# A two-block transformer kernel: the last four meetings of the engines removed, small loads moved

## The chip, the cores and the metric

The kernel runs on one core of a Trainium2 chip. The metric is device time in microseconds of one execution. The core has five engines with queues of their own: TensorE (PE), VectorE (DVE), ScalarE (ACT), GpSimd (POOL) and SyncE (SP, which here issues most of the DMA transfers). They meet only through semaphores.

## What is computed

Two blocks are applied to 512 tokens of width 1024, all in float32. The first block is a token mixer (a gated recurrence and an mLSTM), a cross-attention and a squared-ReLU MLP, then a norm. The second block is cut here to the part around the change; its expert layer follows behind it.

```python
a = rmsnorm_2(h, norm_mix[l])
proj = a @ w_in[l]
aq, ak, av, gq, gk, gv, gr, z_f, z_b, g_att, g_gla = split_columns(proj)
aq = partial_rope(aq.reshape(B, S, ATT_HEADS, ATT_HEAD_DIM), positions)
ak = partial_rope(ak.reshape(B, S, ATT_KV_HEADS, ATT_HEAD_DIM), positions)
y_att = windowed_gqa(aq, ak, av, attn_sink[l]) @ w_branch_attn[l]
y_gla = gla_branch(gq, gk, gv, gr, z_f, z_b, gla_gate_up_fwd[l], ...) @ w_branch_gla[l]
merged = jax.nn.sigmoid(g_att) * y_att + jax.nn.sigmoid(g_gla) * y_gla
h = h + merged @ w_out[l]
```

`partial_rope` turns the first 16 of each head's 64 values by sine and cosine of position times eight frequencies. `z_f` and `z_b` are 16 columns each of the projection; `gla_branch` multiplies them by the small `up` weights, and the result is the log decay of each token.

## The kernel before

**Products and their weights.** Each large product runs over panels of 512 weight columns, and a panel is cut into parts of two row tiles (256 rows, 512 KB). A float32 value is written as an upper part in the matmul's rounded format and a remainder, and a product is three matmuls (upper by upper, upper by remainder, remainder by upper). One part takes 24 matmuls of 128x512. SP loads parts into four raw buffers (`raw`, L2483); a raw buffer is loaded again as soon as its part is split. The split writes the upper half and the remainder into one of two slots. In most stages POOL does both (L580 and L581, in `split_parts_of`). In `proj_h` and `proj_m`, ACT copies the upper half (L590, `split_hi`) and POOL subtracts (L599, `split_lo`). A slot is free when PE has used the part two before. So splitting runs two parts ahead of PE at most, and `early(name)` splits the first two parts of a stage, `rest(name)` the others.

**PSUM banks.** Eight banks carry all results. A table (`STAGES`) gives every result its bank; PE claims it when its former content has been read (`bank_claim`), and an engine that evacuates it waits until it is written. `bank_written` and `bank_done` are these waits alone. Some stages use only the left or only the right four banks, so that weights' products (`product_steps`, one step is one group of a part, six matmuls) can be put between the small matmuls of another stage.

**The norm before the second block** (`final_mix_act`, `final_mix_dve`, `fused_pe`). DVE adds each bank of the MLP's result to X (L485) and multiplies by a gain (L486: both inputs lie in SBUF), ACT squares and sums, DVE scales (L496), PE transposes (L457), ACT and DVE evacuate into the split input XTS. Then follow `proj_a` (queries, keys, values of the attention), the `z` product with the padded and split weights ZWS (L625), eight steps of `proj_g`, six transposes of the turned queries and keys (`turn_qk`, L2003), the attention with the other steps of `proj_g` and `proj_v` between (`attn_pe`: scores L1381, transposes L1387, outputs L1394), the alpha products with `gatt` between (L2013), `yatt`, and the gated linear attention with `proj_r` between (`gla_pe`, L1488 its first product of each chunk).

**The meetings.** `Stages` (L186) is a barrier of PE, ACT, DVE and POOL: each drains its pipeline, raises `stage_end` and waits until all four have come (L194). There are four: after `z`; after `turn_qk`; after the attention; after `yatt`. Between the first two, DVE computes the angles, ACT their sine and the sine of half of them (L2165, L2166), DVE the cosine, then it turns queries and keys. The scratch of this lies where the attention's scores come later.

**POOL's order.** At the start: clear `small` and `ident`, split two parts of `proj_h`, issue four loads of bias rows `bc`, the sink and the positions, set masks, clear WG and issue four loads of four columns each into it, then go on splitting. Before the second block POOL waits until PE has done the last transpose of the norm, clears ZW, issues two loads of 16 columns each into it and two of `up` weights, and then splits `proj_a` (L1909 to L1916). At the meetings it has split two parts of the next stage.

Of the kernel before, what the change touches and what calls it, by code (L numbers as in the profile page):

```python
# [13 lines left out]
ALU = mybir.AluOpType  # L14
ACT = mybir.ActivationFunctionType
# [65 lines left out]
def build(nc, ctx, A, out):  # L81
# [28 lines left out]
    PT = sb("PT", [P, 2, P])  # L110
    bc = sb("bc", [P, 2048])
# [23 lines left out]
    stage_end = sem("stage_end")  # L135
# [47 lines left out]

    met = []

    class Stages:  # L186

        def __init__(self, eng):
            self.eng, self.n = eng, 0
            met.append(self)  # L190

        def __call__(self):
            self.n += 1
            self.eng.drain().then_inc(stage_end, 1)  # L194
            self.eng.wait_ge(stage_end, 4 * self.n)

# [1081 lines left out]
    CS_, SN_ = a.take(ST, 8), a.take(ST, 8)  # L1278
    RT = a.take(4, ST, 8, 8)
    ANG = a.take(4, ST, 8)  # L1280
# [554 lines left out]
    def _(pool):  # L1835
        meet = Stages(pool)
# [61 lines left out]
        pool.wait_ge(S_("wg_in"), 64)  # L1898
# [33 lines left out]
        early("proj_r")  # L1932
        meet()
        rest("proj_r")
# [8 lines left out]
    def _(pe):  # L1943
        meet = Stages(pe)
# [48 lines left out]
        meet()  # L1993
# [11 lines left out]
        meet()  # L2005
        attn_pe(pe, steps)
        meet()
# [11 lines left out]
        meet()  # L2019
# [62 lines left out]
    def _(act):  # L2082
        meet = Stages(act)
# [73 lines left out]
        final_mix_act(act, BASE["down1"])  # L2157
        act.wait_ge(S_("x_final"), 1)
# [3 lines left out]
        meet()  # L2162

        act.wait_ge(S_("ang"), 1)
        act.activation(SN_[:, :, :], ANG[:, 0], ACT.Sin)  # L2165
        act.activation(CS_[:, :, :], ANG[:, 0], ACT.Sin, scale=0.5).then_inc(S_("sin"), 1)  # L2166
# [4 lines left out]
        meet()  # L2171
        attn_act(act)
        meet()
# [13 lines left out]
        meet()  # L2187
        act.wait_ge(S_("x_kept"), 16)
        gla_act(act, link)
# [280 lines left out]
    def _(sp):  # L2470
# [14 lines left out]
        for p in range(late):  # L2485
            load(p)
# [56 lines left out]
```

## Time and profile before

| | us |
|---|---|
| median of three runs | 2175.28 (2175.22 to 2177.37) |
| the profiled execution | 2175.02 |
| its span | 2173.2 |
| PE busy | 1997.0 |
| DVE busy | 784.0 |
| ACT busy | 532.9 |
| POOL busy | 1029.3 |

The times of the profile are those of one execution, counted from the start of its span. A line of the timeline has start, duration, engine, source line, operation, what it writes and reads, and in brackets how long its engine was idle before it and what ended that. A line of the windows has a stretch, its length, the busy time of PE, of its weight loads (PEld), of DVE, ACT and POOL (with instruction counts), then PE's granted clock as a share of full speed, the DMA engines' busy share and GB/s. The list of waits gives who waited for whom, then total, number and longest.

### The profile page before, as it was taken

How to read it: one execution, taken by the hardware profiler on the slowest of the kernel's cores; microseconds unless marked ns; L12 is line 12 of the kernel's file. 1: busy time of each engine (PE TensorE's matmuls, PEld its weight loads, DVE VectorE, ACT ScalarE, POOL GpSimd, SP SyncE). 2: the span in 40 equal slices, each digit the busy share in tenths (PEclk: the TensorE clock that was granted, in tenths of full speed). 3: DMA queues.
4: the chain of work that ended last, by engine and by line, in shares of the span. 5: the costliest groups of instructions: out<-in, count | busy, mean ns of one | idle time of the engine just before them, and what ended most of it. 6: DMA issues, size and time to landing. Idle time of an engine off the chain costs nothing.

```text
span 2173.2 us, 23270 instructions
## 1 busy us (share of the span) xinstructions
PE 1997.0 (92%) x9424; PEld 1449.9 (67%) x9424; DVE 784.0 (36%) x1186; ACT 532.9 (25%) x1119; POOL 1029.3 (47%) x596
## 2 busy tenths in 40 slices
PE   7988997978989999997999999988979999999977
PEld 6877886767778888886766667877854444434436
DVE  1445558442323301424144374553240111111135
ACT  3434436322312100212023242332120000000032
POOL 6786747736466877885643385445600000000015
PEclk9999998999999999998999999999979999999998
DMA  5321112312222333331311122112659999999971
GB/s 159 97 62 36 40 59 78 127 40 87 68 70 76 97 97 97 97 97 57 112 49 59 49 62 83 57 51 67 244 194 387 409 409 409 409 409 409 409 288 58
DMA packets 116922, 334.89 MB, mean 154 GB/s; under 512 B 8145, under 2 KB 9873, under 8 KB 116561
## 3 DMA queue, kind: packets, MB, share of 16 engines
q1 hardware_dynamic: 111904, 319.97, 40.9%
q10 hardware_dynamic: 4128, 11.60, 1.5%
q0 software_dynamic: 784, 1.84, 0.3%
q8 instruction: 75, 1.23, 0.2%
q14 instruction: 31, 0.25, 0.0%
HBM read 327.10 MB, written 6.29 MB: 153 GB/s over the span
## 4 chain that ended last, share of the span: by engine, by line
PE 78%; DVE 6%; POOL 6%; DMA 5%; ACT 3%; issue 2%; POOLq 1%; PEldq 0%; SPq 0%; DVEq 0%; ACTq 0%; PEld 0%
PE bank L556 47%; PE bank L1709 12%; PE bank L1739 3%; PE bank L1726 2%; PE bank L718 2%; POOL shared_r L580 2%; DMA shared<-in_w_exp_gate 2%; POOL shared_r L581 2%; PE bank L457 1%; PE bank L1381 1%; DMA arena<-in_w_exp_up 1%; DMA arena<-in_w_exp_gate 1%; DMA shared<-in_w_exp_down 1%; PE bank L1394 1%; POOL shared_r L599 1%
## 5 line engine op out<-in xcount | busy, mean ns | idle before, releaser
L556 PE MATMUL bank<-shared_r 128*128 128x512 f32 (+1 forms) x4032 | 962.7, 395 | 41.0 <-POOL shared_r L581 18.8
L556 PEld LDWEIGHTS bank<-shared_r 128*128 128x128 f32 x4032 | 746.3, 194 | 217.0 <-issue 26.9
L580 POOL TENSOR_TENSOR shared_r<-shared,small 128x1024 fp32r<-128x1024 f32 (+1 forms) x184 | 355.3, 1931 | 992.3 <-DMA shared<-in_w_ple_gate 530.7
L581 POOL TENSOR_TENSOR shared_r<-shared,shared_r 128x1024 fp32r<-128x1024 f32 (+1 forms) x184 | 455.4, 2475 | 14.5
L648 DVE TENSOR_TENSOR X<-bank,X 128x512 f32<-128x512 f32 x96 | 66.4, 692 | 427.8 <-PE bank L1726 240.8
L1709 PE MATMUL bank<-shared,arena 128*64 128x512 f32 x864 | 191.3, 594 | 10.6 <-DMA shared<-in_w_exp_gate 4.0
L556 PE MATMUL bank<-shared_r,arena_r 128*128 128x512 f32 x768 | 176.1, 391 | 0.0
L556 PEld LDWEIGHTS bank<-shared_r,arena_r 128*128 128x128 f32 x768 | 144.2, 188 | 31.5
L1709 PE MATMUL bank<-arena 128*64 128x512 f32 x672 | 149.2, 594 | 6.6 <-DMA arena<-in_w_exp_gate 2.0
L1709 PEld LDWEIGHTS bank<-shared,arena 128*64 128x64 f32 x864 | 67.4, 137 | 129.7 <-issue 119.9
L599 POOL TENSOR_TENSOR shared_r<-shared,shared_r 128x1024 fp32r<-128x1024 f32 x32 | 80.5, 2516 | 79.8 <-ACT shared_r L590 79.8
L1709 PEld LDWEIGHTS bank<-arena 128*64 128x64 f32 x672 | 51.9, 137 | 98.7 <-issue 90.2
L718 PE MATMUL bank<-arena 128*128 128x64 f32 x448 | 60.9, 286 | 15.9 <-DVE arena L863 12.3
L2155 ACT ACTIVATE arena<-arena 128x512 f32<-128x512 f32 x32 | 20.2, 632 | 224.8 <-DVE arena L2311 224.3
L718 PEld LDWEIGHTS bank<-arena 128*128 128x128 f32 x448 | 60.6, 206 | 19.7 <-DVE arena L863 13.5
L556 PE MATMUL bank<-arena_r,shared_r 128*128 128x512 f32 x288 | 67.7, 395 | 0.8 <-issue 0.8
L1739 PEld LDWEIGHTS bank<-arena 128*128 128x128 f32 x512 | 60.4, 199 | 9.0 <-issue 7.9
L1739 PE MATMUL bank<-arena 128*128 128x128 f32 x512 | 61.7, 284 | 3.0 <-issue 1.9
L556 PEld LDWEIGHTS bank<-arena_r,shared_r 128*128 128x128 f32 x288 | 53.8, 187 | 14.3 <-issue 1.2
L2311 DVE TENSOR_SCALAR arena<-bank 128x512 f32<-128x512 f32 x32 | 21.9, 685 | 113.6 <-PE bank L556 113.2
L1777 ACT ACTIVATE arena<-bank 128x512 f32<-128x512 f32 x16 | 8.8, 595 | 218.3 <-PE bank L1763 218.2
L1726 PE MATMUL bank<-arena 128*128 128x512 f32 x128 | 56.8, 597 | 2.1 <-issue 2.1
(392 smaller groups left out, 2030.2 us busy)
## 6 DMA issues: line engine op xcount, KB each, us to landing
shared<-in_w_in SPq DMA_DIRECT2D x80, 512.0 KB, 3.6
shared<-in_w_exp_up SPq DMA_DIRECT2D x38, 1024.0 KB, 18.3
shared<-in_w_exp_down SPq DMA_DIRECT2D x36, 1024.0 KB, 18.6
shared<-in_w_exp_gate SPq DMA_DIRECT2D x34, 1024.0 KB, 18.2
arena<-in_w_exp_gate SPq DMA_DIRECT2D x30, 1024.0 KB, 18.5
arena<-in_w_exp_down SPq DMA_DIRECT2D x28, 1024.0 KB, 18.3
arena<-in_w_exp_up SPq DMA_DIRECT2D x26, 1024.0 KB, 18.2
shared<-in_w_up SPq DMA_DIRECT2D x32, 512.0 KB, 3.7
```

Of the source, the lines that this page charges most:

```text
L457: ins = pe.transpose(bank[:, j * P:(j + 1) * P], XS[:, j, d * P:(d + 1) * P], ident[:, :])
L556: ins = pe.matmul(dst, W_, x_, start=first, stop=final)
L580: link(pool.tensor_tensor(hi, raw(p), small[:, 18:19].to_broadcast([P, hi.shape[1]]), ALU.add))
L581: pool.tensor_tensor(lo, raw(p), hi.bitcast(F32), ALU.subtract).then_inc(S_("w_split"), 1)
L599: pool.tensor_tensor(lo, raw(p), hi.bitcast(F32), ALU.subtract).then_inc(S_("w_split"), 1)
L648: bank_release(dve.tensor_tensor(xs, bank[:, :], xs, ALU.add), n)
L718: ins = pe.matmul(bank[:, h * 64:(h + 1) * 64], HKL[g % 4][:, h, :], HQL[g % 4][:, h, :], start=True, stop=True)
L1381: ins = pe.matmul(bank[:, lo:hi], QT[r, hp, x * P:(x + 1) * P], KTT[r, g, (x - 1) * P + lo:(x - 1) * P + hi], start=True, stop=True)
L1709: ins = pe.matmul(banks_[h][x_rows(e), :], stay, panel[:, kk, h * 512:(h + 1) * 512], start=k == 0, stop=k == KT - 1)
L1726: bank_ready(pe.matmul(bank[:, :], AOH[i % 2][:, 1, j * P:(j + 1) * P], YP[:, h * 512:(h + 1) * 512], start=True, stop=True), n)
L1739: ins = pe.matmul(bank[:, dd * P:(dd + 1) * P], XS[:, j, d * P:(d + 1) * P], OH[i % 2][:, j].rearrange("p e c -> p (e c)"), start=j == 0, ...
L2311: bank_release(dve.tensor_scalar(HR[:, f % 4, :], bank[:, :], 0.0, None, ALU.max), n)
```

## The change

The four meetings go, with the class. In their place stand single waits: PE waits after `turn_qk` for ACT's six evacuations, after the attention only for the `up` load, and for nothing of its own after `z` and `yatt`. DVE waits for the releases of `proj_a` before it turns, and for PE's last transpose of `turn_qk` before it writes scores. ACT waits for the last two attention outputs before it copies them, and for `ots` before the linear attention. POOL waits for the last transpose of the attention's probabilities before it clears cells of CG; it no longer waits for the norm's transposes.

The padded weights `g_weights` and `z_weights` are written once at launch into arrays of 128 x 1024 with zeros between, and loaded by one transfer each: WG by SP, ZW by ACT behind the norm's evacuations. ACT also issues the two `up` loads, SP the `bc` loads, the sink and the positions, between its fourth and fifth weight part. The sine table has a buffer of its own, `rope`, and is made at the beginning.

```diff
+    rope = sb("rope", [P, 6, ST, 8])
+    CS_, SN_, ANG = rope[:, 0], rope[:, 1], rope[:, 2:6]
...
     @block.gpsimd
         early("proj_h")
-        for i, c0 in enumerate((1536, 2048, 3584, 4096)):
-            pool.dma_start(bc[:, i * 512:(i + 1) * 512], A["b_in"][0, c0:c0 + 512].partition_broadcast(P)).then_inc(S_("bc_in"), 16)
-        pool.dma_start(sink, A["attn_sink_2"][0].partition_broadcast(P)).then_inc(S_("sink_in"), 16)
-        pool.dma_start(pos_i, A["positions_2"].rearrange("a (j p) -> p (a j)", p=P), allow_slow_non_contiguous=True).then_inc(S_("sink_in"), 16)
...
-        link(pool.memset(WG[:, :, :], 0.0))
-        for q in range(4):
-            pool.dma_start(WG[:, :, 32 * q:32 * q + 4], W1[0, :, 4608 + 4 * q:4612 + 4 * q].rearrange("(k p) n -> p k n", p=P)).then_inc(S_("wg_in"), 16)
...
-        bank_written(pool, BASE["norm_mix2"] + KT - 1)
-        link(pool.memset(ZW[:, :, :], 0.0))
-        zc = W2[0, :, 3840:3872].rearrange("(k p) n -> p k n", p=P)
-        for i in range(2):
-            pool.dma_start(ZW[:, :, 32 * i:32 * i + 16], zc[:, :, 16 * i:16 * i + 16]).then_inc(S_("zw_in"), 16)
-        for i, nm in enumerate(("gla_gate_up_fwd_2", "gla_gate_up_bwd_2")):
-            pool.dma_start(UP[32 * i:32 * i + 16, :], A[nm][0]).then_inc(S_("up_in"), 16)
         rest("proj_a", 0)
-        pool.wait_ge(S_("zw_in"), 32)
+        pool.wait_ge(S_("zw_in"), 16)
         split_gates(ZW, ZWS)
-        early("proj_g")
-        meet()
-        split_parts_of(pool, link, "proj_g", skip=2, count=2)
-        pool.wait_ge(S_("up_in"), 32)
-        meet()
-        rest("proj_g", 4)
+        rest("proj_g", 0)
         rest("proj_v", 0)
         early("gatt")
-        meet()
+        bank_written(pool, att_bank["turn", NH - 1, 2])
         for d in range(2):
             pool.memset(CG[:, d, :, :, 0:1], 0.0)
         pool.drain().then_inc(S_("cg_zero"), 1)
         rest("gatt")
         rest("yatt", 0)
-        early("proj_r")
-        meet()
-        rest("proj_r")
+        rest("proj_r", 0)
...
     @block.tensor
         gates_product(pe, ZWS, bank_claim(pe, n), n, 2)
-        meet()
         steps = chain(*(product_steps(pe, PB["proj_g"] + i, XB, fm=i < 2) for i in range(4)))
...
             bank_ready(ins, n)
-        meet()
+        for i in range(6):
+            bank_done(pe, BASE["turn_qk"] + i)
         attn_pe(pe, steps)
-        meet()
+        pe.wait_ge(S_("up_in"), 32)
...
         product(pe, PB["yatt"], [OTS[:, b] for b in range(2)], fm=True)
-        meet()
...
     @block.scalar
         split_hi(act, "proj_h", hi, 6)
+        act.wait_ge(S_("ang"), 1)
+        act.activation(SN_, ANG[:, 0], ACT.Sin)
+        act.activation(CS_, ANG[:, 0], ACT.Sin, scale=0.5).then_inc(S_("sin"), 1)
...
         final_mix_act(act, BASE["down1"])
+        act.dma_start(ZW[:, :, :], A["z_weights"].rearrange("p (k n) -> p k n", k=KT)).then_inc(S_("zw_in"), 16)
+        for i, nm in enumerate(("gla_gate_up_fwd_2", "gla_gate_up_bwd_2")):
+            act.dma_start(UP[32 * i:32 * i + 16, :], A[nm][0]).then_inc(S_("up_in"), 16)
         act.wait_ge(S_("x_final"), 1)
...
-        meet()
         attn_act(act)
-        meet()
+        for h in (NH - 2, NH - 1):
+            bank_done(act, att_bank["out", h, 0])
...
-        meet()
         act.wait_ge(S_("x_kept"), 16)
+        act.wait_ge(S_("ots"), 1)
         gla_act(act, link)
...
     @block.vector
         first_dve(dve, link)
+        dve.wait_ge(S_("sink_in"), 32)
+        link(dve.tensor_copy(pos_f, pos_i))
...
+        dve.sem_inc(S_("ang"), 1)
+        dve.wait_ge(S_("sin"), 1)
+        link(dve.tensor_tensor(CS_, CS_, CS_, ALU.mult))
+        link(dve.tensor_scalar(CS_, CS_, -2.0, 1.0, ALU.mult, ALU.add))
...
-        meet()
+        for n in eight("proj_a"):
+            bank_done(dve, n)
...
         last.then_inc(S_("roped"), 1)
-        meet()
+        bank_written(dve, BASE["turn_qk"] + 5)
         attn_dve(dve, link)
-        meet()
         dve.wait_ge(S_("cg_zero"), 1)
...
-        meet()
         gla_dve(dve, link)
...
     @block.sync
-        for p in range(late):
+        for p in range(4):
+            load(p)
+        for i, c0 in enumerate((1536, 2048, 3584, 4096)):
+            sp.dma_start(bc[:, i * 512:(i + 1) * 512], A["b_in"][0, c0:c0 + 512].partition_broadcast(P)).then_inc(S_("bc_in"), 16)
+        sp.wait_ge(S_("zeroed"), 1)
+        sp.dma_start(sink, A["attn_sink_2"][0].partition_broadcast(P)).then_inc(S_("sink_in"), 16)
+        sp.dma_start(pos_i, A["positions_2"].rearrange("a (j p) -> p (a j)", p=P), allow_slow_non_contiguous=True).then_inc(S_("sink_in"), 16)
+        sp.dma_start(WG[:, :, :], A["g_weights"].rearrange("p (k n) -> p k n", k=KT)).then_inc(S_("wg_in"), 16)
+        for p in range(4, late):
             load(p)
```

## Rows read from the trace of the kernel before

**Rows 1.** Page, busy time, share of the span and instructions of PE and its weight loads

```profile
PE 1997.0 (92%) x9424; PEld 1449.9 (67%) x9424; DVE 784.0 (36%) x1186; ACT 532.9 (25%) x1119; POOL 1029.3 (47%) x596
```

**Rows 2.** Waits of PE, whole run: who for whom, total, times, longest

```profile
PE bank L556 <- POOLq L194: 8.6, 2, 4.6
PE bank L2013 <- POOLq L194: 2.2, 1, 2.2
PE bank L1381 <- POOLq L194: 2.0, 1, 2.0
PE bank L625 <- POOL arena_r L1851: 1.3, 1, 1.3
```

**Rows 3.** Chain that ended last, 0 to 140 us: start, length, engine and line

```profile
19.66 2.27 POOL bc L1859 x4
25.21 3.52 POOL arena L1868 x4
28.74 2.37 POOL shared_r L599
```

**Rows 4.** Windows behind the six gaps of PE and at full clock

```profile
31.15:38.60 7.45, 7.45 (x26) 5.97 (x27) 0.00 (x0) 0.00 (x0) 3.45 (x4) 0.77 0.49 143
38.60:49.45 10.85, 10.85 (x49) 9.01 (x48) 0.00 (x0) 5.83 (x7) 6.98 (x9) 1.00 0.22 55
1028.45:1035.82 7.37, 7.37 (x26) 5.96 (x27) 3.87 (x2) 0.00 (x0) 6.04 (x2) 0.77 0.47 177
1064.82:1070.56 5.74, 5.74 (x24) 4.39 (x24) 0.00 (x0) 0.00 (x0) 5.66 (x3) 1.00 0.10 11
1074.63:1087.95 13.32, 13.32 (x49) 10.75 (x49) 5.97 (x25) 1.63 (x3) 4.29 (x2) 0.81 0.11 37
1092.70:1098.84 6.14, 6.14 (x17) 3.66 (x17) 1.53 (x4) 0.00 (x0) 0.00 (x0) 0.72 0.32 88
1098.84:1103.48 4.64, 4.64 (x17) 2.68 (x16) 1.91 (x3) 0.00 (x0) 0.00 (x0) 1.00 0.00 0
1237.69:1250.25 12.56, 12.56 (x25) 5.98 (x25) 2.25 (x3) 1.89 (x1) 0.17 (x2) 0.59 0.16 43
1250.25:1260.81 10.56, 10.56 (x34) 5.36 (x33) 3.00 (x4) 7.02 (x4) 4.26 (x2) 1.00 0.18 50
1329.04:1336.10 7.06, 7.06 (x25) 5.68 (x26) 2.98 (x5) 4.23 (x14) 0.00 (x0) 0.78 0.27 74
```

**Rows 5.** Timeline of ACT at the start: copies of upper halves

```profile
21.86 1.06 ACT L590 ACTIVATE shared_r<-shared 128x1024 fp32r<-128x1024 f32 x1 [3.52 <-PE bank L556]
49.51 1.06 ACT L590 ACTIVATE shared_r<-shared 128x1024 fp32r<-128x1024 f32 x1 [0.64 <-PE bank L556]
```

**Rows 6.** Timeline at the MLP's norm, first product and third split

```profile
657.25 32.99 PE L556 MATMUL bank<-shared_r 128*128 128x512 f32 x143
663.10 1.89 POOL L580 TENSOR_TENSOR shared_r<-shared,small 128x1024 fp32r<-128x1024 f32 x1 [12.84 <-PE bank L556]
```

**Rows 7.** Timeline around the norm before the second block

```profile
960.77 2.87 DVE L486 TENSOR_TENSOR arena<-X,bc 128x512 f32<-128x512 f32 x1
997.16 1.89 POOL L580 TENSOR_TENSOR shared_r<-shared,small 128x1024 fp32r<-128x1024 f32 x1 [1.12 <-PE bank L556]
1008.76 0.69 DVE L486 TENSOR_TENSOR arena<-X,bc 128x512 f32<-128x512 f32 x1
1028.45 35.10 PE L556 MATMUL bank<-shared_r 128*128 128x512 f32 x192 [9.39 <-POOL shared_r L581]
```

**Rows 8.** Timeline, POOL's second split of proj_g and ACT's evacuations of turn_qk

```profile
1068.96 1.89 POOL L580 TENSOR_TENSOR shared_r<-shared,small 128x1024 fp32r<-128x1024 f32 x1
1088.59 3.04 ACT L2170 ACTIVATE arena<-bank 128x512 f32<-128x512 f32 x6 [10.26 <-PE bank L2003]
```

**Rows 9.** Timeline of POOL at the end of yatt

```profile
1326.59 2.34 POOL L581 TENSOR_TENSOR shared_r<-shared,shared_r 128x1024 fp32r<-128x1024 f32 x1
```

**Rows 10.** DMA issues: the load of the positions, KB and us to landing

```profile
small<-in_positions POOLq DMA_DIRECT2D x1, 2.0 KB, 5.0
```

More of the change, by code:

```diff
@@ L134, in build @@
     raw_full = [sem(f"raw_full{i}") for i in range(4)]
-    stage_end = sem("stage_end")
     sems = {}
@@ L182, in __call__ @@
             return ins
[L184 to L195, printed above, removed]
     panels, parts = [], []
@@ L1277, in build @@
     KDUP = a.take(ST, 2, 2, 64)
-    CS_, SN_ = a.take(ST, 8), a.take(ST, 8)
     RT = a.take(4, ST, 8, 8)
-    ANG = a.take(4, ST, 8)
     OTS = Area(gla_at + 4 * S, arena_r).take(2, 4, S)
@@ L1835, in _ @@
     def _(pool):
-        meet = Stages(pool)
         link = Chain(pool, "pool_own")
@@ L1897, in _ @@
         assert lo_at[0] == 20
-        pool.wait_ge(S_("wg_in"), 64)
+        pool.wait_ge(S_("wg_in"), 16)
         split_gates(WG, WGS)
@@ L1943, in _ @@
     def _(pe):
-        meet = Stages(pe)
         first_pe(pe)
@@ L2082, in _ @@
     def _(act):
-        meet = Stages(act)
         link = Chain(act, "act_own")
@@ L2161, in _ @@
         bank_release(act.activation(ZT[0:48, :], bank[0:48, :], ACT.Copy), BASE["z"])
-        meet()
-        act.wait_ge(S_("ang"), 1)
-        act.activation(SN_[:, :, :], ANG[:, 0], ACT.Sin)
-        act.activation(CS_[:, :, :], ANG[:, 0], ACT.Sin, scale=0.5).then_inc(S_("sin"), 1)
         for i in range(6):
@@ L2240, in _ @@
     def _(dve):
-        meet = Stages(dve)
         link = Chain(dve, "dve_own")
@@ L2249, in _ @@
         first_dve(dve, link)
+        dve.wait_ge(S_("sink_in"), 32)
+        link(dve.tensor_copy(pos_f, pos_i))
+        link(dve.tensor_tensor(ANG[:, 0], pos_f.unsqueeze(2).to_broadcast([P, ST, 8]), invf.unsqueeze(1).to_broadcast([P, ST, 8]), ALU.mult))
+        link(dve.tensor_scalar(ANG[:, 1], ANG[:, 0], float(1 / (2 * np.pi)), None, ALU.mult))
+        link(dve.tensor_copy(ANG[:, 2].bitcast(I32), ANG[:, 1]))
+        link(dve.tensor_copy(ANG[:, 1], ANG[:, 2].bitcast(I32)))
+        c1 = 6.28125
+        c2 = float(np.float32(np.round((2 * np.pi - c1) * 2 ** 21) / 2 ** 21))
+        c3 = float(2 * np.pi - c1 - c2)
+        for c in (c1, c2, c3):
+            link(dve.scalar_tensor_tensor(ANG[:, 0], ANG[:, 1], -c, ANG[:, 0], ALU.mult, ALU.add))
+        link(dve.tensor_scalar(ANG[:, 0], ANG[:, 0], 3.1415925, -3.1415925, ALU.min, ALU.max))
+        dve.sem_inc(S_("ang"), 1)
+        dve.wait_ge(S_("sin"), 1)
+        link(dve.tensor_tensor(CS_, CS_, CS_, ALU.mult))
+        link(dve.tensor_scalar(CS_, CS_, -2.0, 1.0, ALU.mult, ALU.add))
         for i in range(8):
@@ L2332, in _ @@
             bank_release(dve.tensor_copy(AKV[:, j, :], bank[:, 0:256]), n)
-        meet()
-        link(dve.tensor_copy(pos_f, pos_i))
-        link(dve.tensor_tensor(ANG[:, 0], pos_f.unsqueeze(2).to_broadcast([P, ST, 8]), invf.unsqueeze(1).to_broadcast([P, ST, 8]), ALU.mult))
-        link(dve.tensor_scalar(ANG[:, 1], ANG[:, 0], float(1 / (2 * np.pi)), None, ALU.mult))
-        link(dve.tensor_copy(ANG[:, 2].bitcast(I32), ANG[:, 1]))
-        link(dve.tensor_copy(ANG[:, 1], ANG[:, 2].bitcast(I32)))
-        c1 = 6.28125
-        c2 = float(np.float32(np.round((2 * np.pi - c1) * 2 ** 21) / 2 ** 21))
-        c3 = float(2 * np.pi - c1 - c2)
-        for c in (c1, c2, c3):
-            link(dve.scalar_tensor_tensor(ANG[:, 0], ANG[:, 1], -c, ANG[:, 0], ALU.mult, ALU.add))
-        link(dve.tensor_scalar(ANG[:, 0], ANG[:, 0], 3.1415925, -3.1415925, ALU.min, ALU.max))
-        dve.sem_inc(S_("ang"), 1)
-        dve.wait_ge(S_("sin"), 1)
-        link(dve.tensor_tensor(CS_[:, :, :], CS_[:, :, :], CS_[:, :, :], ALU.mult))
-        link(dve.tensor_scalar(CS_[:, :, :], CS_[:, :, :], -2.0, 1.0, ALU.mult, ALU.add))
+        for n in eight("proj_a"):
+            bank_done(dve, n)
         for x, nh in ((AQ, 8), (AKV[:, :, 0:128].rearrange("p j (h x) -> p j h x", h=2), 2)):
             t1, t2 = x[:, :, :, 0:8], x[:, :, :, 8:16]
-            cs = CS_[:, :, :].unsqueeze(2).to_broadcast([P, ST, nh, 8])
-            sn = SN_[:, :, :].unsqueeze(2).to_broadcast([P, ST, nh, 8])
+            cs = CS_.unsqueeze(2).to_broadcast([P, ST, nh, 8])
+            sn = SN_.unsqueeze(2).to_broadcast([P, ST, nh, 8])
             r = [RT[:, i, :, 0:nh, :] for i in range(4)]
@@ L2393, in _ @@
             bank_release(dve.tensor_tensor(MERGED[:, i, :], bank[:, :], MERGED[:, i, :], ALU.mult), n)
-        meet()
         gla_dve(dve, link)
@@ L2503, in _ @@
         sp.wait_ge(S_("stored"), 16 * ST)
-    assert len({m.n for m in met}) == 1, [m.n for m in met]
     assert split_turn[0] == split_count
@@ L2536 @@
         cols[32 * q:32 * q + 4, 1, P - 1] = arrays["in_b_in"][0, 4608 + 4 * q:4612 + 4 * q]
+    gw, zw = (_np.zeros((P, KT, P), _np.float32) for _ in range(2))
+    for q in range(4):
+        gw[:, :, 32 * q:32 * q + 4] = arrays["in_w_in"][0, :, 4608 + 4 * q:4612 + 4 * q].reshape(KT, P, 4).transpose(1, 0, 2)
+    for i in range(2):
+        zw[:, :, 32 * i:32 * i + 16] = arrays["in_w_in_2"][0, :, 3840 + 16 * i:3856 + 16 * i].reshape(KT, P, 16).transpose(1, 0, 2)
+    for name, a in (("g_weights", gw), ("z_weights", zw)):
+        arrays[f"in_{name}"] = a.reshape(P, KT * P)
+        args[name] = nc.dram_tensor(f"in_{name}", (P, KT * P), _mybir.dt.float32, kind="ExternalInput").ap()
     arrays["in_columns"] = cols.reshape(P, 2 * P)
```

## The prediction

> **What bounds the kernel now.** I read the page first. TensorE (PE) is busy for 92% of the span [rows 1], so a change elsewhere pays only where it closes a gap of PE or raises PE's clock. Next I read the list of waits for PE [rows 2]: 8.6 us in two gaps, 2.2 us and 2.0 us are put down to L194, the wait inside a meeting; a gap of 1.3 us before the `z` product waits for the split of the gate weights and is not touched. Then the timeline around `norm_mix2`, where the longest gap, 9.39 us, lies behind GpSimd's (POOL's) weight split at L581 [rows 7]. Last I read the chain in order of time for the first 140 us: from 19.66 us on it runs through POOL's DMA issues and then through a late split [rows 3]. That makes six gaps of PE: A at 27.20 us (start), B at 1019.06 (before `proj_a`), C at 1070.56 (first meeting), D at 1090.73 (second), E at 1235.45 (third), F at 1324.46 (fourth).
>
> **The clock behind each gap.** The windows [rows 4] show the granted clock after the gaps: 0.72 to 0.81 in five of them and 0.59 in E, which is a stretch at 1.2 GHz and the rest at 2.4 GHz. Two parts of weights (48 matmuls) take 10.85 us at full clock, so one part takes 5.44. After A the same part takes 7.45 (a few tens of ns of it belong to the next), a loss of 2.0. After B it takes 7.37: 1.9. After C two parts take 13.32 against 10.85: 2.5. In F 7.06 against 5.44: 1.6. In D two rounds of one score and one step take 6.14, where two such rounds at full clock take 4.64: 1.5. In E three rounds of one alpha and one step take 12.56, while four take 10.56 just behind them: 12.56 - 7.92 = 4.6. The 1.3 us gap before `z` is followed by clock 1.00 and 5.74 us for its 24 matmuls [rows 2, 4]. So I take it that a gap of about one microsecond leaves the clock alone, and that one of two or more lowers it.
>
> **A, the start.** POOL leaves its second split at 19.66 us, issues four `bc` loads (2.27) and two small ones (1.3), does memsets (1.7), issues four `WG` loads (3.52) and only at 28.74 starts the split that PE waits for from 27.20 to 31.15 [rows 3]. ACT had the upper half ready at 21.86 + 1.06 = 22.92 [rows 5]. Without the issues and the `WG` memset POOL is free at about 20.5, starts at 22.95 and ends at 25.3, 1.9 us before PE asks. The next copy waits for PE to use a buffer, so its split ends 3.6 us after 27.2, again 1.8 ahead of need. The gap is gone: 3.95 + 2.0 of clock = 5.9.
> What is moved: seven DMA issues go to SP, between its fourth and fifth weight load. The fifth load waited until 15.3 for its buffer anyway, and the part that it carries is wanted only at about 32.6. Eleven small instructions of DVE and three of ACT move to the start. DVE has nothing to do there until the second panel of `proj_h` is done, eight parts of 5.44 after PE's start at about 16, so they cost nothing. ACT does the two sines in 1.63 us including a table load (the x3 in the C window [rows 4]) ahead of the evacuation of `proj_h`. The copy of ACT that follows those evacuations had 0.64 us of idle time before it [rows 5], so it comes 1.0 us late; its split then ends at 53.1 + 1.0 where PE asks at 54.9, in the times of before. Cost nothing, with 0.8 to spare.
> A rule speaks against this term. The Trainium skill (DMA: Bandwidth & Descriptors, "Issuing engines are not separate DMA queues") says that issuing from another engine saves only the sequencer's issuing time, usually small beside the transfer. By it alone A would be near nothing and the sum 28.2 instead of 34.1; the chain shows that here the issuing time itself is what ends last.
>
> **B, before proj_a.** POOL waits until PE has done the norm's last transpose, then memset, four issues and two splits: PE stands 9.39 us [rows 7]. Without this wait POOL splits both parts while the norm runs, as it does at the MLP's norm: there POOL is done with both 12.84 us before 663.10, at 650.3, and the product follows the transposes at 657.25 with no gap [rows 6]. Gain 9.3 + 1.9 of clock = 11.2.
> But these splits now run beside a chain that PE waits for. L486 (two SBUF inputs) takes 0.69 us alone and 2.87 us beside POOL; it ends about 0.55 after the POOL instruction ends [rows 7]. POOL's splits keep a step of 5.49, so the first starts at 997.16 + 5.49 = 1002.65 with its second half at 1004.62, and the second split starts at 1008.1 and ends at 1012.8. The four L485/L486 pairs come 1.37 apart, the first L486 at 1004.64, the last ending at 1009.45 [rows 7]. If POOL is first at 1004.62, the L486 end at 1007.6, 1010.55, 1013.4 and 1014.8: 5.3 later. If DVE is first, they end at 1005.3, 1008.0, 1010.5 and 1013.4: 3.9 later. The rest of the norm follows at the same distance. The starts lie 20 ns apart, so I take the middle, 4.6. B = 11.2 - 4.6 = 6.6, with 5.9 and 7.3 as near ends and 11.2 if nothing collides.
> The Trainium skill (SBUF — State Buffer, "Who interferes with whom") has this as a rule: a VectorE instruction with two SBUF inputs and a GpSimd one that reads SBUF exclude each other for a whole instruction. The row agrees; without it the sum would be 38.7.
>
> **C, first meeting.** The meeting waited for POOL's second split of `proj_g`. The first one ends when its successor starts, at 1068.96 [rows 8], before `z` ends at 1070.56 (1064.82 + 5.74 [rows 4]). So PE goes on at once: 4.07 (8.6 less F's 4.58) + 2.5. DVE's rope work without the sines is 14 instructions, about 4 us of the 5.97 in that window [rows 4]. It now starts near 1064 and shares boundaries with POOL. That may lengthen POOL's splits by some 0.35 each; I take off 0.2. The table is wanted 10.9 us after `z`. C = 6.4.
>
> **D, second meeting.** PE now waits for ACT's six evacuations, which end at 1088.59 + 3.04 = 1091.63 [rows 8], 0.9 after PE's last transpose. 1.97 becomes 1.0, and such a gap kept the clock before `z`. D = 1.0 + 1.5 = 2.5, or 1.0 if the clock falls all the same.
>
> **E, third meeting.** The first alpha product needs a bank that ACT has already freed. PE goes on at 1235.5. POOL came last to this meeting, at 1237.69 (start of the E window [rows 4]), with a split of `gatt`; its memsets and `cg_zero` still follow that split, so DVE's first evacuation can't start before 1238, 1.5 after the product it empties. Four banks cover 7.9 us of PE, so this costs nothing. E = 2.2 + 4.6 = 6.8 [rows 2, 4], or 2.2.
>
> **F, fourth meeting.** PE waited until POOL had split two parts (1326.59 + 2.34 = 1328.93 [rows 9]); the first was ready at 1323.4. PE goes on at 1324.5, and the first `own` product, at 1336.10 before (end of the last window of rows 4), comes after 5.44. DVE's memset and first products now meet POOL's split and end at about 1330.2, 0.3 after PE asks. F = 4.6 + 1.6 - 0.3 = 5.9, down to 5.0.
>
> **Sum.** 5.9 + 6.6 + 6.4 + 2.5 + 6.8 + 5.9 = 34.1. The profiled execution took 2175.02 (span 2173.2), the median is 2175.28, so they need no correction: 2175.3 - 34.1 = 2141.2 us. The stretches between the gaps wait only for their own predecessors and should move as blocks.
>
> **Rivals.**
> *The thin stretches stay slow.* The work behind D and E is thin (alpha products with 16 rows, scores with 64), and E's low stretch is the longest, though its gap is short. If the thin work and not the gap lowers the clock, 1.5 + 4.6 are not won: 2147.3. Against it: the attention stage, as thin, runs at full clock up to 1235. Chance 0.2.
> *No collision in B.* DVE and POOL slip past each other: 2136.6. Against: the 2.87 us row. 0.1.
> *POOL takes the place of the meetings.* Splits of 4.3 us for parts of 5.44 leave it 1.1; if DVE's work holds it for one instruction of 2.4 in each of B, C, D and F, PE waits 9.6 in all: 2150.8. 0.1.
> *The start gains nothing.* The loads put between the weights hold the third part's data back past 25 us: 2147.1. Against: they are queued behind it. 0.07.
> *Slower.* ACT's wait for the angles stands before every later copy of the `proj_h` weights, and the angles wait for the position and sink loads. They landed 5.0 us after issue from POOL [rows 10]. If they land on SP's queue after about 37 us, every microsecond holds ACT, POOL and PE; the change is slower than before from about 71 us on, and at 80 us it is 2184. Nothing in the trace is near that. 0.03.
>
> **How the numbers follow.** The forecast has 0.5, with its own range 2137 to 2145. The range 2132 to 2154 takes in the rivals but the last, with some room for blocks that don't move quite together. This kernel can be told from no change at 0.2%, 4.3 us: faster 0.94, same 0.03, slower 0.03.
>
> **What would show it.** A: PE's line L556 without a gap at 27, clock 1.00 from 16 us on. B: the first `proj_a` matmul within 0.2 us of the last transpose, PE's wait for L496 longer by 4 to 5 us, an L486 of over 2 us behind 1003. C, E, F: no wait put down to L194 and clock 1.00 behind them. D: a gap of 1.0 that ACT L2170's line ends. Low clock behind E, or new waits for L581, would prove the first or third rival.

## The result and the profile after

The changed kernel takes 2142.74 us (median of 6 runs, 2138.09 to 2146.39); the kernel before, timed beside it, takes 2176.32. The ratio is 0.9844, 95% interval 0.9828 to 0.9860: faster by 1.6%. The forecast was 2141.2 with a range of 2132 to 2154. The profiled execution took 2142.04 with a span of 2140.3, against 2173.2 before: 32.9 us less.

The page's busy time of the changed kernel, which answers to [rows 1]:

```profile
PE 1983.9 (93%) x9424; PEld 1441.6 (67%) x9424; DVE 797.5 (37%) x1186; ACT 532.3 (25%) x1119; POOL 1018.2 (48%) x580
```

PE is 13 us less busy for the same 9424 matmuls: that part of the gain is clock. DVE is 13.5 us more busy for the same 1186 instructions; the splits that now run beside it, shown below, are the likely reason, but their share of it was not added up. The waits of PE in the changed kernel (who for whom, total, times, longest), which answer to [rows 2]:

```profile
PE bank L441 <- DVE arena L480: 9.9, 1, 9.9
...
PE bank L609 <- POOL arena_r L1832: 1.2, 1, 1.2
PE bank L1363 <- ACT arena L2128: 1.1, 1, 1.1
```

The meeting's line is gone; 1.1 us behind ACT's evacuations stands where the second meeting had 2.0, the wait before `z` stays, and the one big wait, 9.9 us for the norm's scaling L480, was 4.7 before. The windows of the changed kernel (us, busy time of PE, PEld, DVE, ACT and POOL with instructions, PEclk, DMA share, GB/s) answer to [rows 4]: the norm's transposes, `proj_g` behind `z`, 10 us behind the first long pause of the attention stage, and three rounds of `alpha`.

```profile
1012.18:1017.39 5.21, 5.21 (x32) 5.21 (x33) 4.16 (x8) 3.56 (x6) 0.00 (x0) 0.65 0.00 0
1058.23:1069.12 10.89, 10.89 (x49) 8.96 (x48) 5.77 (x11) 0.59 (x1) 7.65 (x4) 1.00 0.33 95
1106.70:1116.78 10.08, 10.08 (x36) 6.78 (x37) 1.66 (x3) 0.00 (x0) 0.00 (x0) 0.66 0.13 48
1215.94:1223.82 7.88, 7.88 (x25) 4.02 (x24) 2.95 (x4) 1.91 (x1) 2.34 (x3) 1.00 0.25 69
```

`proj_g` takes 10.89 us where it took 13.32, three `alpha` rounds 7.88 where they took 12.56. In the third line the clock is low although nothing was changed there.

To see where 32.9 us went I cut PE's timeline into blocks at six starts that both kernels have: the norm before the MLP, the norm before `proj_a` (L441), `z` (L609), the first score (L1363), and the first and last `out` step of attention (L1376). The table holds the distance from each start to the next in every trace of this case. Its first column is the start of the norm before the cross attention (from there to the norm before the MLP it is 130.2 to 130.3 us in every trace), its last runs from the last `out` step to the norm before the router. "As changed" is the changed kernel.

```
kernel              start  norm-norm  norm-z   z-score  to out  out-out  to router
before              521.11  361.34    52.10    27.88    35.17   105.18   347.24
as changed          515.35  366.57    40.47    20.40    33.65   106.91   333.78
again               520.13  366.59    40.46    20.41    33.65   106.89   333.78
bc_from_gpsimd      515.96  366.56    40.49    20.40    33.65   106.86   333.80
gates_from_gpsimd   515.87  366.52    40.50    20.43    33.64   106.88   333.76
pause_before_alpha  520.04  366.55    40.51    20.42    33.63   106.90   340.39
sines_late          517.65  366.61    40.50    26.94    33.64   104.11   335.05
meetings_back       518.04  366.59    40.51    24.45    35.21   103.77   347.02
norm_wait_back      520.10  361.43    48.28    20.42    33.64   103.76   334.14
splits_after_recip  516.05  366.89    41.46    20.43    33.64   105.40   333.95
splits_after_norm   515.26  361.39    41.21    20.42    33.63   103.76   334.32
after_norm_5        513.02  361.27    41.27    20.42    33.63   103.75   334.35
gates_in_two        515.35  361.36    41.43    20.32    33.63   103.76   334.28
gates_between       515.31  361.36    40.87    20.34    33.63   108.20   333.87
```

Before to changed: start 5.76, norm to norm -5.23, norm to `z` 11.63, `z` to score 7.48, to the first `out` 1.52, inside attention -1.73, to the router 13.46. The sum is 32.89, the whole change of the span. The first column moves by up to 7 us between kernels that hardly differ up to there ("again" is the changed kernel itself, 4.8 later), so it says little about the start; effects of a few microseconds are read from the other columns. The clock moves it. In every trace PE waits 2.17 us near 140 us. From that wait's end to the end of the next, of 2.12, PE runs the same instructions in every trace, and the stretch takes 15.97 us in seven traces, 17.6 in four, 19.16 in meetings_back and 20.7 in norm_wait_back and pause_before_alpha. The changed kernel shows two of these values in its two traces, first here and then in "again" (PE alone: length, busy time, granted clock, DMA share, GB/s):

```profile
139.79:155.76 15.97, 13.85 (x91) 1.00 0.00 1
```

```profile
141.98:159.54 17.56, 15.44 (x90) 0.90 0.00 1
```

Whether this also makes up the spread of 8 us among the runs of the changed kernel is not shown, since only the profiled runs have a trace.

### The profile page after: what moved, and what is told of

Its sections match the earlier page's. It is cut to its first block, busy times and chain, and to the rows that moved or that the text cites. A ratio compares the mean times of both kernels' runs of the same rounds, so it can differ in the third digit from the quotient of the medians.

```text
span 2140.3 us, 23254 instructions
## 1 busy us (share of the span) xinstructions
PE 1983.9 (93%) x9424; PEld 1441.6 (67%) x9424; DVE 797.5 (37%) x1186; ACT 532.3 (25%) x1119; POOL 1018.2 (48%) x580
## 4 chain that ended last, share of the span: by engine, by line
PE 80%; DVE 7%; DMA 5%; POOL 4%; ACT 3%; issue 2%; PEldq 0%; DVEq 0%; ACTq 0%; PEld 0%; SPq 0%; POOLq 0%
PE bank L540 48%; PE bank L1691 12%; PE bank L1721 3%; PE bank L1708 2%; PE bank L702 2%; DMA shared<-in_w_exp_gate 2%; PE bank L441 1%; POOL shared_r L565 1%; POOL shared_r L564 1%; PE bank L1363 1%; DMA arena<-in_w_exp_up 1%; PE bank L1376 1%; DMA arena<-in_w_exp_gate 1%; DMA shared<-in_w_exp_down 1%; DVE arena L1625 1%
## 5 line engine op out<-in xcount | busy, mean ns | idle before, releaser
L540 PE MATMUL bank<-shared_r 128*128 128x512 f32 (+1 forms) x4032 | 952.5, 392 | 19.2 <-POOL shared_r L565 9.5
L565 POOL TENSOR_TENSOR shared_r<-shared,shared_r 128x1024 fp32r<-128x1024 f32 (+1 forms) x184 | 456.1, 2479 | 14.4
L702 PEld LDWEIGHTS bank<-arena 128*128 128x128 f32 x448 | 60.6, 207 | 19.7 <-DVE arena L847 13.5
```

Of the source, the lines that this page charges most:

```text
L540: ins = pe.matmul(dst, W_, x_, start=first, stop=final)
L565: pool.tensor_tensor(lo, raw(p), hi.bitcast(F32), ALU.subtract).then_inc(S_("w_split"), 1)
L702: ins = pe.matmul(bank[:, h * 64:(h + 1) * 64], HKL[g % 4][:, h, :], HQL[g % 4][:, h, :], start=True, stop=True)
```

## The experiments

**again**: the changed kernel itself.

> The changed kernel once more, for a second trace. If it is chance where the low-clock stretch begins behind the 2.7 us gap of the attention stage (before the step at 1106.7 us), that stretch costs another amount here and the 1.7 us given back in that stage come out between 0 and 2; if the change itself costs them (other phase of the engines), the stage is as long as in the first trace to 0.2 us. Time 2142.7 either way, within 1.5.

It took 2144.86 us (4 runs, 2143.60 to 2146.35). Attention, first to last `out`, 106.89 against 106.91: in two traces of the same kernel, 4.8 us apart in time by then, it gives back the same.

**splits_after_norm** and **splits_after_recip**: the two parts of `proj_a` split later.

```
+        pool.wait_ge(S_("fused_xs"), 2 * fth("n5"))   # splits_after_norm
+        pool.wait_ge(S_("fused_r"), fth("n5"))        # splits_after_recip
         rest("proj_a", 0)
```

> GpSimd waits until VectorE has scaled the norm's rows before it splits the two parts of proj_a. Theory (splits and VectorE's products of two SBUF inputs exclude each other): the four L470 take 0.69 us each again, PE's transposes come 5.2 us earlier, the first split ends within 0.5 us of the last transpose: 2137.5 us. Rival (the pairs' distance is set by something else, as the additions L469 or ScalarE's squares): the transposes stay where they are and the first split ends late, so 2143 or more.

> The same wait, one step earlier: GpSimd starts when VectorE has the reciprocal, so its splits run beside the six scalings with one SBUF input. If only two SBUF inputs collide, the scalings keep their 2.47 us and the time is that of splits_after_norm or up to 0.5 better (2137.3). If any SBUF operation of VectorE collides, the six scalings take over 4 us and the transposes come 2 to 3 us later than in splits_after_norm: 2140.

Measured: 2135.29 us (4 runs; ratio to before 0.9813, 0.9793 to 0.9833) and 2145.85 (0.9859, 0.9845 to 0.9874). DVE in the norm (start, length, line; idle time before it and what ended it), first the changed kernel, with POOL's splits between:

```profile
998.89 2.94 DVE L470 TENSOR_TENSOR arena<-X,bc 128x512 f32<-128x512 f32 x1
1002.47 2.37 DVE L470 TENSOR_TENSOR arena<-X,bc 128x512 f32<-128x512 f32 x1
1005.47 2.12 DVE L470 TENSOR_TENSOR arena<-X,bc 128x512 f32<-128x512 f32 x1
1008.23 0.69 DVE L470 TENSOR_TENSOR arena<-X,bc 128x512 f32<-128x512 f32 x1
1010.85 2.47 DVE L480 TENSOR_SCALAR arena<-arena,small 128x512 f32<-128x512 f32 x6
...
998.87 2.41 POOL L565 TENSOR_TENSOR shared_r<-shared,shared_r 128x1024 fp32r<-128x1024 f32 x1
1002.39 1.89 POOL L564 TENSOR_TENSOR shared_r<-shared,small 128x1024 fp32r<-128x1024 f32 x1 [1.11 <-PE bank L540]
1004.37 2.68 POOL L565 TENSOR_TENSOR shared_r<-shared,shared_r 128x1024 fp32r<-128x1024 f32 x1
```

splits_after_norm, two L470, POOL's first split and PE:

```profile
998.84 0.69 DVE L470 TENSOR_TENSOR arena<-X,bc 128x512 f32<-128x512 f32 x1
1002.95 0.69 DVE L470 TENSOR_TENSOR arena<-X,bc 128x512 f32<-128x512 f32 x1
...
1008.12 1.89 POOL L564 TENSOR_TENSOR shared_r<-shared,small 128x1024 fp32r<-128x1024 f32 x1 [12.39 <-DVE arena L480]
...
1006.91 6.31 PE L441 MATMUL bank<-ident,arena 128*128 128x128 f32 x32 [4.72 <-DVE arena L480]
1012.98 33.89 PE L540 MATMUL bank<-shared_r 128*128 128x512 f32 x192
```

splits_after_recip:

```profile
1006.48 10.02 DVE L480 TENSOR_SCALAR arena<-arena,small 128x512 f32<-128x512 f32 x6
...
1006.53 1.89 POOL L564 TENSOR_TENSOR shared_r<-shared,small 128x1024 fp32r<-128x1024 f32 x1 [9.89 <-DVE small L476]
```

Three of the four L470 start while a POOL instruction runs, two of them only 20 and 80 ns behind its start, and each ends about half a microsecond behind that split's end (998.87 + 2.41 = 1001.28 against 1001.83). With the splits later all are back at 0.69 and the norm block is 5.2 us shorter. The product then starts without a gap behind the transposes. In splits_after_recip, L480 reads one tensor in SBUF and a scalar column, and it takes 10.02 us for 2.47, worse than both theories. So "two SBUF inputs" is too narrow, and the 2145.85 us fit neither forecast.

The Trainium skill (SBUF — State Buffer, "Who interferes with whom") has it wider: a `tensor_scalar` from SBUF to SBUF can run in a mode that takes both port pairs, and then it too excludes GpSimd. The traces agree: alone, an L480 takes 2.47 / 6 = 0.41 us for the 512 columns that cost L470 0.69, and beside POOL it waits.

**after_norm_5**: the better of the two in five rounds.

> splits_after_norm once more, in five rounds. Theory: of its gain over the changed kernel the norm block holds 4.4 us (transposes 5.3 earlier, 1.1 lost again to the clock in them, 0.2 gained behind them), the rest of the first median was the attention stage's clock: 2138.3, ratio to the kernel before 0.982. Rival: the attention stage loses nothing whenever the norm runs without the collision: 2135.3, ratio 0.981, and the profile has clock 1.00 behind the gap before L1376 again.

Measured: 2133.53 us (5 runs, 2132.55 to 2137.51), ratio to before 0.9816, 0.9800 to 0.9831. Attention took 103.75 us again, as the rival said. But the interval takes in both forecasts, 0.982 and 0.981, and the rival's rule, that attention loses nothing whenever the norm runs without the collision, falls with gates_between below: no collision there, and attention took 108.20.

**norm_wait_back**: POOL waits for the norm's last transpose again.

```
+        bank_written(pool, BASE["norm_mix2"] + KT - 1)
         rest("proj_a", 0)
```

> GpSimd waits again until PE has done the norm's last transpose before it splits proj_a's first two parts; the loads of the gate weights stay with ScalarE. Theory: the collision of the norm goes (transposes 5.2 us earlier), a gap of one split (1.9 + 3.3 us) comes behind them and the clock behind it costs 1.9, so proj_a ends about 2 us later than in the changed kernel: 2144.8. Of B's 6.4 us, then, two thirds came from the memset and the four DMA issues that left GpSimd's way, and one third from the wait. Rival (the wait carries all of B): 2149.1.

Measured: 2142.77 us (4 runs, 2138.85 to 2146.73), ratio 0.9859 (0.9842 to 0.9876), not to be told from the changed kernel. By the table the norm is 5.14 shorter and the way to `z` 7.81 longer, 2.67 in all (2.0 expected). Attention takes 3.15 less, which hides it in the median. PE in it:

```profile
1011.83 6.31 PE L441 MATMUL bank<-ident,arena 128*128 128x128 f32 x32 [4.72 <-DVE arena L480]
1023.48 35.38 PE L540 MATMUL bank<-shared_r 128*128 128x512 f32 x192 [5.34 <-POOL shared_r L565]
```

So of B's 6.40 us (11.63 - 5.23) the wait holds 2.67. The other 3.7 are the difference, and go to the memset and the four DMA issues that left POOL's way.

**gates_between** and **gates_in_two**: on top of splits_after_norm the split of the `z` gates comes earlier, whole between `proj_a`'s fourth and fifth part, or one instruction behind the second part and one behind the fourth.

```
@@ gates_between
+        split_parts_of(pool, link, "proj_a", count=4)
         pool.wait_ge(S_("zw_in"), 16)
         split_gates(ZW, ZWS)
+        rest("proj_a", 4)
@@ gates_in_two
+        link(pool.tensor_tensor(ZWS[:, 0], zw, ..., ALU.add))
+        split_parts_of(pool, link, "proj_a", skip=2, count=2)
+        pool.tensor_tensor(ZWS[:, 1], zw, ZWS[:, 0].bitcast(F32), ALU.subtract).then_inc(S_("gates_split"), 1)
+        rest("proj_a", 4)
```

> As splits_after_norm, and the split of the z gate weights stands between the fourth and the fifth part of proj_a, where GpSimd is idle for 1.5 us and has 5.4 us per part. Theory: the 1.25 us gap before z goes, the fifth part is ready 0.2 us before PE asks, clock stays 1.00: 2136.3. Rival (it only moves the gap to the second panel, whose parts are short, 2.9 us each, for 2.45 us of splitting): a gap of 0.5 to 1.5 us appears in the second panel, 2137.5.

> As splits_after_norm, and the two instructions of the z gate split stand apart: the first behind proj_a's second part (2.0 us idle), the second behind its fourth (0.6 idle and more slack behind). Theory: no gap before z and none in the second panel; z starts 1.2 us after what splits_after_norm had less 2.4, at 1046.9, and the time is that of splits_after_norm less 1.2, give or take the 0 to 4.4 us that the attention stage draws. Rival (the gate weights land too late for the second part's place, or the fifth part comes late): a gap of over 0.3 us in proj_a and z no earlier than 1047.8.

Measured: 2138.49 us (0.9830, 0.9815 to 0.9844) and 2135.49 (0.9830, 0.9815 to 0.9844). The wait before `z` goes in both, and another comes inside `proj_a`. PE of gates_between, then of gates_in_two:

```profile
1036.21 11.76 PE L540 MATMUL bank<-shared_r 128*128 128x256 f32 x96 [0.81 <-POOL shared_r L565]
1047.80 5.66 PE L609 MATMUL bank<-shared_r,arena_r 128*128 128x512 f32 x24
```

```profile
1025.89 22.68 PE L540 MATMUL bank<-shared_r 128*128 128x512 f32 x144 [1.67 <-POOL shared_r L565]
1048.41 5.66 PE L609 MATMUL bank<-shared_r,arena_r 128*128 128x512 f32 x24
```

Against splits_after_norm the way from the norm to `z` is 0.3 shorter in the first and 0.2 longer in the second. Both theories failed and both rivals held: a gap of 0.81 in the second panel, where 0.5 to 1.5 was said, and one of 1.67 inside `proj_a` with `z` at 1048.41, where over 0.3 and no earlier than 1047.8 was said. The main reason is another than the rivals gave: I gave POOL 4.3 us per split, and behind the norm DVE's last products L485 stretch the third and fourth to between 5.2 and 6.1. There POOL, not the order of its work, sets the pace. gates_between also lost 4.4 us in attention.

**bc_from_gpsimd** and **gates_from_gpsimd**: the start's loads back on POOL, one half each. The first issues `bc`, `sink` and the positions there, the second makes the memset and the four gate loads there. The second expectation was written for a kernel with both halves; the kernel that ran has the gate half alone, so it tests no combination.

```
+        for q in range(4):      # gates_from_gpsimd, behind memset(WG)
+            pool.dma_start(WG[:, :, 32 * q:32 * q + 4], ...)
```

> In the changed kernel the four bc loads and the two small ones are issued by GpSimd again, at their old place; the gate weights still come padded and whole over the SP queue. Theory: of A's 3.95 us gap 3.75 go with the 5.3 us of memset and gate loads alone: GpSimd starts the split at 25.0 and ends it at 27.4, PE waits 0.2 us, no clock is lost, 2143 as the changed kernel. Rival (the issues of bc are what ends last): a gap of over 2 us at 27 and 2 more of clock, 2147.

> The counterpart of bc_from_gpsimd with both halves back: bc, the two small loads, the memset of the gate weights and their four loads are all issued by GpSimd as before. Theory: the gap of 3.9 us at 27 comes back, with a low-clock stretch worth 0 to 2.0: A is 3.9 to 5.9 us, 2147 to 2149 if the attention draws as in the changed kernel. Rival (SP's loads between the weights, not GpSimd's issues, decide): no gap of over 2 us at 27.

Measured: 2144.65 us (0.9867, 0.9853 to 0.9882; 4 runs of 2142.51 to 2146.34), and 2142.54 in one run. POOL and PE of the first, then of the second:

```profile
24.64 2.39 POOL L583 TENSOR_TENSOR shared_r<-shared,shared_r 128x1024 fp32r<-128x1024 f32 x1 [0.71 <-ACT shared_r L574]
...
16.07 24.10 PE L540 MATMUL bank<-shared_r 128*128 128x512 f32 x98 [1.84 <-DVE shared_r L623]
```

```profile
25.15 2.41 POOL L583 TENSOR_TENSOR shared_r<-shared,shared_r 128x1024 fp32r<-128x1024 f32 x1
...
27.61 20.70 PE L540 MATMUL bank<-shared_r 128*128 128x512 f32 x90 [0.53 <-POOL shared_r L583]
```

With 3.6 us of `bc` and small issues back there is no gap, with 4.7 us of memset and gate loads back 0.53. Together they had cost 3.95. The split had room of 1.6 us (23.15 + 2.40 = 25.55 in the changed kernel, against about 27.1), and each half alone nearly fits in it. No run has both halves back with everything else as changed.

**sines_late**: angles and sines at their old place.

```
@@ scalar, start
-        act.wait_ge(S_("ang"), 1)
-        act.activation(SN_, ANG[:, 0], ACT.Sin)
...
@@ scalar, behind the evacuation of z
+        act.wait_ge(S_("ang"), 1)
+        act.activation(SN_, ANG[:, 0], ACT.Sin)
...
@@ vector, behind the evacuation of proj_a instead of at the start
+        link(dve.tensor_copy(pos_f, pos_i))
...
```

> The angles and the two sines are worked out at their old place, behind proj_a's evacuation, with nothing else changed. Theory (5 us of cover: in the changed kernel the rope work ends at 1064.1 and PE asks at 1069.1): the sines wait for the evacuation of z at 59.0, are done at 61, and the rope work that follows has GpSimd's pause of 2.3 us for itself; it ends at 1068 to 1069.6, PE waits 0 to 0.5 us, 2143. Rival (the place of the table carries part of C): a gap of 2 us or more before the transposes, with its clock, 2146 or more.

Measured: 2151.10 us, one run; `z` to score 26.94 against 20.40. My theory fell. DVE and PE:

```profile
1054.16 0.77 DVE L2291 CAST small<-small 128x4 f32<-128x4 int32 x1
1054.96 1.84 DVE L2292 TENSOR_TENSOR rope<-small 128x32 f32<-128x32 f32 x1
1056.84 0.18 DVE L2293 TENSOR_SCALAR rope<-rope 128x32 f32<-128x32 f32 x1
1057.05 2.27 DVE L2294 CAST rope<-rope 128x32 int32<-128x32 f32 x1
...
1076.82 4.15 PE L1961 MATMUL bank<-ident,arena 128*128 128x128 f32 x24 [5.13 <-DVE arena L2322]
1081.99 0.67 PE L1363 MATMUL bank<-arena 64*128 64x256 f32 x2 [1.02 <-ACT arena L2128]
```

An instruction on 32 columns takes 0.18 us when POOL is idle and up to 2.27 beside a split; the nine of the angles take 10.0 us (1054.16 to 1064.15). Before, they ran in 1.9 us (1074.61 to 1076.55) while POOL stood still: with both parts split for the meeting, it waited for PE to free a slot until 1082.84. So with the meetings gone the move of the table is worth 6.5 us of the 7.5 that this block won, and without it the first meeting's end would have been worth 1. The two do not simply add up: with the meetings there the table's move is worth 3.4 (24.45 in meetings_back, the next run, against 27.88).

**meetings_back**: the four meetings and POOL's order around them, in the changed kernel.

```
-        rest("proj_g", 0)
+        early("proj_g")
+        meet()
+        split_parts_of(pool, link, "proj_g", skip=2, count=2)
+        meet()
+        rest("proj_g", 4)
...
```

> The four meetings, with GpSimd's order of splits around them, come back; start, norm and sine table stay as changed. Theory: PE's stages C to F take the 22.1 us longer that the two traces show (6.7, 2.3, 7.0, 6.1), less what the attention stage draws for its clock (0 to 4.4 us in the five traces so far, 3.1 in the changed kernel): 2164.8, between 2161.5 and 2166. Rival (part of the gain is that the sine table no longer stands between the meetings): C comes back with less than 6 us and the time is below 2160.

Measured: 2163.48 us (6 runs, 2149.33 to 2168.52), ratio to before 0.9947 (0.9918 to 0.9976). PE behind the four meetings:

```profile
1064.08 11.19 PE L554 MATMUL bank<-shared_r 128*128 128x512 f32 x48 [2.93 <-POOLq L196]
...
1079.85 1.16 PE L1377 MATMUL bank<-arena 64*128 64x256 f32 x2 [1.96 <-POOLq L196]
...
1223.48 2.07 PE L1995 MATMUL bank<-arena 16*128 16x512 f32 x2 [2.25 <-POOLq L196]
...
1314.75 7.36 PE L554 MATMUL bank<-shared_r 128*128 128x512 f32 x24 [4.58 <-POOLq L196]
```

The gaps of D, E and F return to within 0.05 us of [rows 2], and the last column to 0.2. The median is near the forecast, but its six runs spread over 19 us, and the one with a trace took 2158.04, so the blocks say more. C is not as forecast: a gap of 2.93 for 4.07, and the product behind it at full speed (11.19 for 13.32). `z` to `out` grows by 5.6, not 9.0. The rival was right that C would return with less than 6, and its time, below 2160, holds for the traced run but not for the median. Its reason is not shown by this: the missing part lies in the gap and in the clock behind it, and PE waits for the rope work in neither kernel.

**pause_before_alpha**: PE waits for ACT's copy of the attention's output.

```
         pe.wait_ge(S_("up_in"), 32)
+        pe.wait_ge(S_("ot_hi"), 1)
```

> PE waits before the first alpha product until ScalarE has copied the attention's output, which nothing else needs there: a pause of about 2.7 us where the third meeting had 2.2. Theory (a pause of two to three microseconds costs its length and a low-clock stretch that in the traces so far was worth 0 to 4.6 us): the stage is 2.7 to 7.3 us longer, 2145 to 2150. Rival (the prediction's rule, that such a pause always lowers the clock): 4.6 of clock as before, 2150. Rival (the meeting itself and not the pause brought the low clock): 2.7 and clock 1.00.

Measured: 2153.50 us, one run, 4.7 of it in the first column. PE:

```profile
1223.57 1.09 PE L1973 MATMUL bank<-arena 16*128 16x512 f32 x2 [2.83 <-issue]
1224.59 2.34 PE L540 MATMUL bank<-shared_r 128*128 128x512 f32 x6
1226.86 2.07 PE L1973 MATMUL bank<-arena 16*128 16x512 f32 x2
1228.86 2.93 PE L540 MATMUL bank<-shared_r 128*128 128x512 f32 x6
```

The last column grows by 6.6: 2.9 for the pause, 3.1 for the clock up to the first `own` product (90.75 against 87.62 us from the first `alpha`), the rest later. Here the first two `alpha` matmuls still ran at full speed (1.09 us) and the low stretch came behind them. The range for the stage (2.7 to 7.3) held, the one for the time (2145 to 2150) did not, by the first column, and the rule of a fixed 4.6 fell too. The pause alone brings the low clock, with no meeting.

## Why the prediction was right

**A**, 5.9 said, 5.85 measured. The first column's 5.76 is too loose to show it: with the trace of "again" it would be 0.98, and the whole gain 28.6 for 32.9. That the two traces compared here had the same clock behind the pause near 140 us (15.97 us in both) was luck. A firmer measure ends at the wait of 0.94 us for POOL's split later in `proj_h` (at 99.50 us before, 93.77 now): from PE's first product to there it is 83.43 us before and 77.54 to 77.58 in ten traces with the changed start. "again" and bc_from_gpsimd need 79.2, since there the clock was low for the first 6 us (0.71 in 16.07 to 22.00 of the latter) though no wait of PE for POOL came before it. The gap is gone (the window of PE's first 44 us, busy all through), and POOL starts the split when ACT has the half:

```profile
23.15 2.40 POOL L583 TENSOR_TENSOR shared_r<-shared,shared_r 128x1024 fp32r<-128x1024 f32 x1 [2.63 <-ACT shared_r L574]
...
16.19:60.22 44.03, 44.03 (x194) 36.46 (x195) 9.06 (x21) 15.05 (x20) 25.67 (x29) 1.00 0.40 112
```

The two halves taken alone show the slack.

**B**, 6.6 said, 6.40 measured. The collision was worth 5.23, inside 3.9 to 5.3; gap and clock gave 11.63, where 11.2 was said. POOL and DVE started within 20 ns of each other as computed, POOL first, and that branch came out: its ends gave L470 of 3.0, 2.3, 2.2 and 0.7 us and 5.3 in all, and 2.94, 2.37, 2.12 and 0.69 were measured. The sum had taken the middle of both branches, 4.6, so it had this term 0.6 too small, and gap and clock 0.4 too small, which offset each other. splits_after_norm shows that the collision was avoidable: with a wait that ends when DVE is done, PE has the first part in time all the same.

**C and D**, 6.4 + 2.5 = 8.9 said, 7.48 + 1.52 = 9.00 measured; by the start of `turn_qk` C is 6.66 and D 2.34. The sum was right, but a reason for it was thin. I called the sine table's move free and took no gain for it. sines_late shows that it is needed for 6.5 of this, because the same work beside POOL's splits takes 10 us.

**E and F**, 6.8 + 5.9 = 12.7 said, 13.46 measured up to the router; by the first `alpha` and `own` starts E is 7.0 and F 6.1. Together the six steps came to 34.4 for 34.1.

**What failed** is the step "the stretches between the gaps should move as blocks". Attention took 1.73 us more. The gap of 2.72 us before its first `out` step is the same in every kernel; the clock behind it is not. The first `out` step in the changed kernel, in after_norm_5, in gates_between, and in the kernel before:

```profile
1106.70 3.31 PE L1376 MATMUL bank<-arena 128*64 128x128 f32 x20 [2.72 <-ACT arena L1406]
```

```profile
1099.83 2.37 PE L1376 MATMUL bank<-arena 128*64 128x128 f32 x20 [2.73 <-ACT arena L1406]
```

```profile
1101.77 4.50 PE L1376 MATMUL bank<-arena 128*64 128x128 f32 x20 [2.73 <-ACT arena L1406]
```

```profile
1127.87 3.79 PE L1394 MATMUL bank<-arena 128*64 128x128 f32 x20 [2.72 <-ACT arena L1424]
```

Over the whole stage that is 3.2, 0, 4.4 and 1.4 us above the shortest. Five traces whose PE does the same from the norm on agree to 0.05 us, though they come there up to 5 us apart in time; the five at 103.8 have another norm, or the meetings. So the price of a pause isn't a constant of the gap. That it depends on what PE did before fits these traces, but it can't be the whole of it: behind the pause near 140 us the price differs by up to 4.8 us though PE had run the same instructions, and by 1.6 between the two traces of the changed kernel. The rule that I took from five gaps ("two or more lowers the clock") is too simple: a pause of 2.7 cost nothing in five of the traces, and 2.93 before `proj_g` cost 0.14 (11.03 us to the first `turn_qk` transpose against 10.89). What sets it was not found; it repeats in attention and not at the start.

The rival of thin stretches is refuted: without a gap the `alpha` rounds run at clock 1.00 (7.88 us). POOL did not take the meetings' place: PE's waits for L565 are 9.5 us where those for L581 were 18.8, and the 9.4 of B are the difference. Nothing was late at the start.

Three points stay open: what sets the clock behind a pause, and with it most of the first column's 7 us; why the first meeting alone ended 1.36 us behind POOL's split (1073.27, PE on at 1074.63) while in meetings_back it ended 0.2 behind (1063.87, 1064.08); and how much of the spread among untraced runs is the clock.

## What to carry to other kernels

Before letting two engines overlap, list the instructions of VectorE that touch SBUF on both sides beside a GpSimd split: small ones suffer most, 0.18 us becoming 2. A barrier that keeps GpSimd still may be what makes such a chain short, so move the chain out before the barrier goes. A wait for the end of the critical chain (here the norm's scaling) can be better than none: splits_after_norm is 0.3% faster than the changed kernel (0.9816 against 0.9844 of before; the intervals, 0.9800 to 0.9831 and 0.9828 to 0.9860, just overlap, so the medians alone don't prove it, but from the norm before the MLP to `z` it is 4.4 us shorter by the blocks). Read effects of a few microseconds from distances between fixed points of the trace, and price the clock behind a pause as a range, here 0 to 4.8 us.

## What was not expected of the hardware

A `tensor_scalar` with one SBUF tensor is held up by GpSimd (2.47 to 10.02 us for six), and so are casts on 32 columns (0.18 to 2.27). A pause of PE of 2.7 us in attention is followed by anything from no low-clock stretch at all (granted clock 1.00 over the whole stage in after_norm_5) to one that costs 4.4 us. There it is the same to 0.05 us in five traces with the same work; a pause of 2.17 us near the start is not the same in two traces of one kernel. And behind the norm's longer gap (9.93 us for 4.7) the transposes were faster, 5.21 us at a granted clock of 0.65 against 6.07 at 0.56 in splits_after_norm, whose window is:

```profile
1006.91:1012.98 6.07, 6.07 (x32) 6.07 (x33) 4.88 (x8) 4.09 (x7) 4.78 (x3) 0.56 0.00 0
```
